# Products that nobody reads, put on TensorE in front of its waits, in a two-model transformer kernel

## The reference, cut to what matters

```
first block, for l in 0, 1:
    z   = x @ w_in[l] + b_in[l]                       # pool, sparse attention, memory attention, gates
    mix = (gated sum of the three branches) @ w_out[l]
    x   = layer_norm(alpha * x + mix)
    x   = layer_norm(alpha * x + moe(x))              # 16 experts, 2 per token
second block, for l in 0, 1:
    z2  = rms(x) @ w_in_2[l]
    x   = x + concat(window attention, forgetting attention, mlstm) @ w_out_2[l]
    x   = x + square(relu(rms(x) @ w_ff1_2[l])) @ w_ff2_2[l]
```

## Time and profile before

| | us |
|---|---|
| median of 3 runs (lowest to highest) | 1998.13 (1995.09 to 2003.88) |
| the profiled execution, its own time | 1996.95 |
| its span, first to last instruction | 1995.5 |
| PE busy in the span | 1706.3 |
| DVE busy, ACT busy | 778.8, 668.6 |

### The profile page before, as it was taken

The page is one execution under the profiler, slowest core; times in us unless marked ns, Lnnn a source line. Parts: engine busy times, 40 slices in busy tenths (PEclk is TensorE's granted clock), DMA queues, the critical chain, the costliest instruction groups (busy, mean ns, idle before and its releaser), DMA issues.

```text
span 1995.5 us, 22133 instructions
## 1 busy us (share of the span) xinstructions
PE 1706.3 (86%) x9214; PEld 1268.4 (64%) x9214; DVE 778.8 (39%) x1480; ACT 668.6 (34%) x1077; POOL 29.5 (1%) x49
## 2 busy tenths in 40 slices
PE   6998987799887998987799985858899998588999
PEld 5777885443335777885443334744699887447997
DVE  4545343310115545343211015642455555515554
ACT  3336421111114336422111114442444444415443
POOL 4000000000000000000000000000000000000000
PEclk9998998799997999998799997976899998678999
DMA  8332445499994432345599992500255544003552
GB/s 260 131 126 103 148 148 211 183 421 421 421 420 174 145 125 105 148 148 211 195 421 421 421 421 106 199 30 1 104 184 187 176 145 176 0 21 127 190 190 105
DMA packets 57663, 392.67 MB, mean 197 GB/s; under 512 B 7124, under 2 KB 7168, under 8 KB 15696
## 3 DMA queue, kind: packets, MB, share of 16 engines
q1 hardware_dynamic: 54144, 380.30, 49.9%
q0 software_dynamic: 3264, 9.61, 1.5%
q10 hardware_dynamic: 144, 1.24, 0.2%
HBM read 390.07 MB, written 1.05 MB: 196 GB/s over the span
## 4 chain that ended last, share of the span: by engine, by line
PE 73%; DVE 10%; DMA 10%; ACT 5%; issue 2%; SPq 0%; DVEq 0%; ACTq 0%
PE psum L547 70%; DMA ring_sb<-in_weights 10%; PE psum L673 2%; ACT ring_rounded L1141 1%; DVE ring_rounded L1493 1%; PE psum L592 1%; ACT region_sb L1167 1%; DVE x_sb L1604 0%; ACT xT_hi_rounded L1376 0%; DVE x_sb L1602 0%; DVE region_sb L1881 0%; DVE region_sb L1884 0%; DVE small_sb L1877 0%; DVE region_sb L1875 0%; DVE small_sb L1590 0%
## 5 line engine op out<-in xcount | busy, mean ns | idle before, releaser
L547 PE MATMUL psum<-ring_sb,region_sb 128*64 128x512 f32 (+1 forms) x1728 | 433.4, 602 | 38.4 <-DMA ring_sb<-in_weights 24.4
L1493 DVE TENSOR_TENSOR ring_rounded<-ring_sb,ring_rounded 128x2048 fp32r<-128x2048 f32 (+4 forms) x152 | 321.4, 2131 | 243.9 <-ACT ring_rounded L1141 243.9
L547 PE MATMUL psum<-xT_hi_rounded,ring_rounded 128*128 128x256 f32 x1920 | 356.4, 287 | 0.0
L547 PEld LDWEIGHTS psum<-ring_sb,region_sb 128*64 128x64 f32 (+1 forms) x1728 | 151.1, 144 | 299.2 <-issue 282.2
L1141 ACT ACTIVATE ring_rounded<-ring_sb 128x2048 fp32r<-128x2048 f32 (+4 forms) x152 | 268.1, 1781 | 210.0 <-PE psum L547 148.8
L547 PE MATMUL psum<-ring_rounded,xT_hi_rounded 128*128 128x384 f32 (+4 forms) x960 | 277.9, 367 | 36.6 <-DVE ring_rounded L1493 17.6
L547 PE MATMUL psum<-xT_lo_rounded,ring_rounded 128*128 128x256 f32 x960 | 285.3, 297 | 27.8 <-DVE ring_rounded L1493 16.8
L547 PEld LDWEIGHTS psum<-xT_hi_rounded,ring_rounded 128*128 128x128 f32 x1920 | 306.8, 196 | 1.8 <-issue 0.5
L547 PEld LDWEIGHTS psum<-ring_rounded,xT_hi_rounded 128*128 128x128 f32 x960 | 184.1, 198 | 61.5 <-issue 39.7
L547 PEld LDWEIGHTS psum<-xT_lo_rounded,ring_rounded 128*128 128x128 f32 x960 | 188.9, 197 | 31.4 <-issue 18.1
L547 PE MATMUL psum<-ring_rounded,region_rounded 128*128 128x512 f32 x768 | 178.7, 392 | 3.0 <-DVE region_rounded L2083 3.0
(11 more groups left out here) (245 smaller groups left out, 1349.1 us busy)
## 6 DMA issues: line engine op xcount, KB each, us to landing
ring_sb<-in_weights SPq DMA_DIRECT2D x324, 1024.0 KB, 8.7
ring_sb<-in_weights SPq DMA_DIRECT2D x24, 768.0 KB, 4.3
ring_sb<-in_weights SPq DMA_DIRECT2D x8, 904.0 KB, 4.6
ring_sb<-in_weights SPq DMA_DIRECT2D x8, 900.0 KB, 4.6
ring_sb<-in_weights SPq DMA_DIRECT2D x8, 584.0 KB, 14.8
region_sb<-in_mem POOLq DMA_DIRECT2D x2, 1024.0 KB, 8.6
region_sb<-in_pool_band POOLq DMA_DIRECT2D x2, 1024.0 KB, 10.1
region_sb<-in_ln_g POOLq DMA_DIRECT2D x4, 512.0 KB, 4.7
```

The lines of the kernel that those rows point to most:

```text
L547: return nc.tensor.matmul(dst, lhsT, rhs, start=first, stop=last, skip_group_check=True)
L1493: nc.vector.tensor_tensor(rounded(piece.raw), piece.raw, reread(piece.hi), ALU.subtract).then_inc(lo_made, 1)
```

## The change

`pe_busy(products, banks)` is added, and called at 22 places of the code. It looks up the bank that the next user of the group will take, waits until that bank's last reader is done, and issues `products` fp32 products of `ident` with the first 256 columns of `upto` into it, each overwriting the last. No semaphore is signalled and no engine reads the result. Nothing else is changed. In the program's order that makes 349 products in 42 groups: 63 and 81 in the two layers of the first block, 115 and 90 in those of the second.

```
+    def next_free(self):
+
+        i = (self.turn + 1) % self.count
+        return self.first + i, self.freed.get(i, (self.full[i], 0))
...
+        def pe_busy(products, banks=None):
+
+            i, free = (banks or loose).next_free()
+            pe.wait_ge(*free)
+            for _ in range(products):
+                matmul(psum[:, i, 0:S], ident, upto[:, 0, :], True, True)
...
             pe.wait_ge(consts_in, 16)
+            if l:
+                pe_busy(18)
             pe_turn_x(l, 0, [x_normed.at(l - 1, 2 + b) if l else (x_in, 32) for b in range(TB)])
+            pe_busy(6)
             cut(0)
...
+            pe_busy(8)
             pe_turn(("q", l), turned, 512, [qT_made.at(l, n) for n in range(2)], q_roped.at(l, 1))
...
+            pe_busy(3)
             pe_turn_probs(("mem_probs", l, 0), mem_probs, MEM_HEADS, TB, [mem_turned.at(l, n) for n in range(2)], mem_shared.at(l, 0))
...
             pe_merge(l, 0, 4)
+            pe_busy(3)
...
+            pe_busy(14)
             pe_held(l, "mixed", xT, [merged_lo.at(l, c) for c in range(4)])
...
+            pe_busy(12)
             pe_turn_x(l, 1, [x_normed.at(l, b) for b in range(TB)])
+            pe_busy(2)
...
+            pe_busy(10)
             i, free, full = loose.take(("order", l), slots_made.at(l, 0))
...
+            pe_busy(5)
             pe_dispatch(l, 0)
...
+            if l == 0:
+                pe_busy(18)
             pe_turn_rms(l, 0, [ff_added.last(l - 1)] if l else [x_normed.at(first_layers - 1, 3)])
+            pe_busy(12 if l == 0 else 5)
             cut(0)
...
             cut(3)
+            pe_busy(10)
...
             cut(5)
+            pe_busy(6, dense)
...
+            pe_busy(7, dense)
             pe_mls_gates(l, 0)
+            pe_busy(24, dense)
             pe_turn(("fox_q", l), fox["turned"], 256, [fox_qk_made.at(l, 0)], fox_normed.last(l))
...
+            pe_busy(5, dense)
             pe_turn_probs(("mls_probs", l, 0), mls["probs"], MLSTM_HEADS, 1, [mls_turned.at(l, 0)], mls_scored.at(l, 3))
...
+            pe_busy(3, dense)
             pe_mls_values(l, 0)
...
+            pe_busy(2, dense)
             pe_fox_scores(l, 1)
+            pe_busy(2, dense)
             pe_turn_probs(("mls_probs", l, 1), mls["probs"], MLSTM_HEADS, 2, [mls_turned.at(l, 1 + n) for n in range(2)], mls_scored.at(l, 7))
             pe_mls_values(l, 1)
+            pe_busy(9, dense)
...
             pe_turn_rms(l, 1, [res_added.at(l, 2 * half + b) for half in range(2) for b in range(TB)])
+            pe_busy(17)
```

5 lines of the change are left out of this document (added).

## The result

| | median us (lowest to highest) | runs |
|---|---|---|
| before | 1997.39 (1995.09 to 2003.88) | 4 |
| changed | 1973.16 (1971.86 to 1976.48) | 4 |

What follows compares the result with a forecast made beforehand. PE was taken to bound the kernel, slowed by half-clock stretches after waits. Terms of 14.7, 13.5 and 31.8 us summed to 60.0, less 8: 1996.95 - 52 = 1945 us; forecast case 1925 to 1968, stated range 1919 to 1978.

Steps and rivals of the forecast that it cites:

- transposes count for nothing: Rival: the clock falls in transposes behind most groups; only `w_out`, dispatch and feed-forward gain; 1991 us, chance 0.07 with other no-difference causes.
- One sign of being right: Second block's attentions: the stretch of 41 us at half clock is gone or is one short piece.
- 8 in front of the `q` transposes: 5.46 / 2 = 2.7 us: First block: half the PE work in the half-clock stretch is gained, 2.7 us in layer 0 and 1.7 in layer 1.
- They cost nothing where they end before the wait behind them does: Price of the products: those finishing within the following wait are free, as 8 products take 3.4 us against 4.58.
- Net 7.2: Second block's 41 us stretch, per layer: 12.4 us gained less 5.2 us for 12 products without their own wait.
- The gross gain: Second block's 41 us stretch, per layer: 12.4 us from PE work at full clock, before the 12 products' cost.
- The 3, 3 and 14: First block: 3 and 3 give 3.4 us per layer; 14 before `w_out` give 2.9 in layer 0, 2.7 in layer 1.
- Route, and start, 10, 6, 7 and 24 of the second block: Per layer: router 2.5, expert order and dispatch 3.2; second block's start 1.5, then 1.7, 2.6 and 0.8 us.
- 17 in front of the feed-forward: Second block, per layer: half of 4.18 us of PE work at half clock is gained, 2.1 us.
- The start of layer 1: First block: 18 and 6 products could gain 4.7 us, but the 18 start late behind the branch; net 0.
- The 8 us taken off: Deducted from the 60.0 us sum because products leave up to 3 us of some waits open and the clock can fall.
- The slow rival: Products neither lift nor hold the clock and outlast the waits; 61 us lost, nothing gained, 2058 us; chance 0.05.

Runs made afterwards that it cites:

- products in the real waits: Changed kernel with the 8 between `q` and `k`, no 5, 3, 2, 2, plus 6 before `fox_probs` and 4 before `fox_out` of phase 0: 1947.95 us.
- the last version: Changed kernel: 8 between `q`/`k`, no 5/3/2/2, 6 and 4 at `fox` waits, 7 for 9, 6 for 18, 9 before `dc == 6`, 5 in feed-forward: 1935.46 us.
- the one-row kernel: Changed kernel with all 349 products using one row of the array instead of 128, same places and columns: 2086.09 us, ratio 1.0455.

## Why the prediction was wrong where it was

**The lever was right.** PE's clock cost time, products hold it up, the mean clock went over 0.96, and the 12.5 us waits are gone. Products with the identity do count: from 604.0 to 614.8 PE ran nothing else, and the clock rose from half to full at 610.0. The rival "transposes count for nothing" had most half-clock stretches stay and 1991 us; 347.5 us at half clock became 116.6, so it didn't come, though no run tests transposes by themselves. One sign of being right didn't come: the 41 us stretch is neither gone nor one short piece, but three, 17 us together. The Trainium skill ("TensorE: Matmul & The Clock Gate", Part 4) says that the full clock doesn't engage for transposes. These products aren't transposes but products with the identity, and they lifted the clock from 0.50 to 1.00 at 610.0.

**Failed: "8 in front of the `q` transposes: 5.46 / 2 = 2.7 us".** It measured -3.4 in layer 0 (from +0.8 at 57.9 to -2.7 at the rope) and -3.5 in layer 1. "They cost nothing where they end before the wait behind them does" was said of 3.4 us against the 4.58 of the earlier trace rows. But that row is of the `k` transposes. Both turns have one line, L592, and I joined the wait to the first. Moved by one turn, the products are worth 3.3 us for both layers, of 4.4 forecast: the term's size was near, its place was wrong.

**Failed: "Net 7.2" for 5, 3, 2, 2 and 9.** It measured -4.8 and -3.2. The text saw that the 12 have no wait of their own and priced them at 5.2 us. It took for granted that they would hold the clock all the same. They don't, for two reasons. The wait of 3.2 us stays open beside them, and the clock falls behind it, at 1333.6. And it falls with no wait in front. At 1319.9 PE had been busy for 6.72 of the 6.80 us before, from 1316.66 on with products on 64 and 8 rows. At 1347.2 it had been busy for all of the last 3.4 us, with products on 64 and 8 rows again. The windows of the changed kernel just ahead of these two falls:

```profile
1316.50:1319.90 3.40, 3.35 (x21) 2.40 (x20) 2.15 (x13) 0.68 (x2) 0.00 (x0) 1.00 0.00 0
1343.80:1347.20 3.40, 3.40 (x12) 1.68 (x12) 0.97 (x2) 0.00 (x0) 0.00 (x0) 1.00 0.01 2
```

The first of them costs time ahead of all 12 products. The 32 products of the window attention's values ran at full clock in before and run at half now (before, then changed):

```profile
1340.51 2.02 PE L547 MATMUL psum<-region_sb 128*64 128x128 f32 x32
1321.69 3.73 PE L552 MATMUL psum<-region_sb 128*64 128x128 f32 x32
```

The same holds in layer 1. The prediction halved half-clock time and had no term for time at full clock that would become half. Then the products themselves run at half clock: the 5 took 3.10 us, not 2.15, and the wait behind them was still whole (the changed kernel's timeline):

```profile
1325.36 3.10 PE L552 MATMUL psum<-consts_sb 128*128 128x256 f32 x10
...
1334.04 1.12 PE L685 MATMUL psum<-consts_sb,xT_hi_sb 128*128 128x128 f32 x4 [3.22 <-DVE xT_hi_sb L1568]
```

The gross gain, forecast at 12.4, was too high as well. With products in the real waits the two stretches gave +4.1 and +3.0, and +8.6 and +6.6 in the last version. The code of these parts differs between the two only by the 7 instead of 9; what the rest of that difference is stays open. In layer 0 the last version is 4.7 us ahead before it reaches the first of these waits, where both have the same code: those 32 products ran at full clock in it (2.02 us) and at half in the other (3.74).

**Held.** The 3, 3 and 14: the parts that hold them gave 4.5 and 5.4 for 6.3 and 6.1. Route, and start, 10, 6, 7 and 24 of the second block: within 2 us in each row of the table. 17 in front of the feed-forward: 1.8 and 1.9 for 2.1. The start of layer 1: the 18 stand behind the branch (3.98 us of "issue") and eat what the clock gives, -0.5 for 0 (-4.2, then +3.8). That they could be six wasn't seen.

**The 8 us taken off** for clocks that still fall were too few: 116.6 us at half clock are left.

**The slow rival** was priced at 2058 for products that neither lift nor hold the clock, and the one-row kernel comes closest to that case: 2086. (Its own price had a slip: 17 products at 0.86 are 14.6 us, 6.2 more than the 8.4 us wait and not 3.8, which makes it 2063.) The two 41 us stretches lose 24 us each in it, where the 24 and the 12 were priced at 8.1 and 10.3.

## What to carry to other kernels

Filler on an engine whose clock follows its activity belongs directly in front of the instruction that waits, and behind whatever that wait itself hangs on (the read that frees a shared tile, the release that starts a transfer); one group of transposes too early it is plain added work. A wait isn't all that lets the clock fall: runs of products on 64 and 8 rows did it too, with PE busy, and filler in the waits leaves those stretches as they are. When two waiting steps have one source line, look up in the timeline which of them has the wait. Sum a change up part by part over an engine whose instructions didn't change: here a total of 20 us hid 14 us of losses in four parts, all of which could be taken back.

## What the runs showed of the hardware

The clock's support by filler goes by the rows of the array that it uses: 0.971, 0.935 and 0.896 with 128, 64 and one row, for the same columns and the same spacing of the records. With 64 rows, PE was busy with these products for 15.67 of 15.70 us and the clock stayed at half. So a busy PE is not enough for the full clock.

That fits the falls inside the second block's attentions, as in the changed kernel's stretch with 6.90 of 6.90 us busy at half clock, where most products use 8 or 64 rows or 64 columns of the array. For the 64 rows the filler shows it apart from the rest. What the 8 rows and the 64 columns do by themselves no run here separates. Nor is it shown whether the rows count or the data in them: the products with fewer rows also read less of the identity.
